# Two decode-state decays move from VectorE to GpSimd in a hybrid decoder step

## What is computed

```
# mixer A (HGRN2), one token per request
S_new = exp(b_last)[..., None] * S + einsum('bshk,bshv->bhkv', k * exp(b_last[:, None] - b), v)
# mixer B (mLSTM, the matrix memory)
a_c   = exp(F[:, -1] + m - m_new)
C_new = a_c[..., None, None] * C + einsum('bshk,bshv->bhkv', k * w[..., None], v)
n_new = a_c[..., None] * n + sum(k * w[..., None])
```

## Time and profile before

| | us |
|---|---|
| median of three runs | 1974.56 (1973.75 to 1975.65) |
| the profiled execution | 1974.06 |
| span of the profiled execution (first to last instruction) | 1972.0 |
| TensorE busy (89% of the span) | 1749.7 |
| VectorE busy (49%) | 960.1 |
| ScalarE busy (35%) | 693.6 |
| GpSimd busy (20%) | 386.5 |
| mean granted clock of TensorE | 0.903 of full |

### The profile page before, as it was taken

How to read it: one execution, slowest core, us unless ns; L and a number is a source line. 1 busy time by engine, 2 the same in 40 slices (tenths; PEclk the granted TensorE clock), 3 DMA queues, 4 the chain that set the end, 5 groups by cost and what they waited for, 6 DMA issues and landing times.

```text
span 1972.0 us, 33878 instructions
## 1 busy us (share of the span) xinstructions
PE 1749.7 (89%) x13564; PEld 1652.9 (84%) x13564; DVE 960.1 (49%) x1457; ACT 693.6 (35%) x1046; POOL 386.5 (20%) x234
## 2 busy tenths in 40 slices
PE   6999977579999999998999784776999999999994
PEld 6998945378999999998998562676999999999993
DVE  4676464542221122226764636335465465465484
ACT  4533353033221122235333431353344344344342
POOL 4302501033434343542015000203000000000031
PEclk8999975589999999999999755787999999999997
DMA  4212225022232222222123000237786786786782
GB/s 166 86 65 93 87 94 234 24 90 75 87 103 80 83 90 94 85 88 68 64 93 98 34 1 0 92 127 239 245 289 215 251 288 218 246 290 217 246 324 71
DMA packets 69274, 268.23 MB, mean 136 GB/s; under 512 B 11252, under 2 KB 11988, under 8 KB 68348
## 3 DMA queue, kind: packets, MB, share of 16 engines
q1 hardware_dynamic: 61152, 242.05, 35.8%
q10 hardware_dynamic: 4348, 15.89, 2.4%
q0 software_dynamic: 3648, 8.53, 1.2%
HBM read 250.09 MB, written 36.29 MB: 145 GB/s over the span
## 4 chain that ended last, share of the span: by engine, by line
PE 82%; DVE 10%; ACT 3%; issue 3%; DMA 1%; ACTq 1%; POOL 0%; DVEq 0%; POOLq 0%; SPq 0%
PE psum L1143 38%; PE psum L1190 11%; PE psum L1667 11%; PE psum L1677 10%; PE psum L1669 8%; PE psum L1195 1%; PE psum L1646 1%; DVE n L1738 1%; ACT a_pb L769 1%; PE psum L1635 1%; DVE r_ee L2132 0%; ACTq L959 0%; DVE r_bt L1934 0%; DVE acc L1725 0%; DVE a_lm L1804 0%
## 5 line engine op out<-in xcount | busy, mean ns | idle before, releaser
L1667 PE MATMUL psum<-xg,xhi 128*128 128x320 f32 x1408 | 376.7, 310 | 1.0 <-issue 0.5
L1669 PE MATMUL psum<-xg,xlo 128*128 128x256 f32 x1408 | 375.1, 281 | 0.0
L594 POOL TENSOR_TENSOR wlo<-wraw,whi 128x1024 fp32r<-128x1024 f32 (+1 forms) x90 | 230.5, 2563 | 349.6 <-ACT whi L730 349.6
L1667 PEld LDWEIGHTS psum<-xg,xhi 128*128 128x128 f32 x1408 | 265.4, 188 | 3.0 <-issue 2.8
L1669 PEld LDWEIGHTS psum<-xg,xlo 128*128 128x128 f32 x1408 | 264.6, 188 | 0.0
L1143 PE MATMUL psum<-xnh,whi 128*128 128x260 f32 x1120 | 234.8, 291 | 31.0 <-POOL xnl L647 13.4
L405 DVE TENSOR_TENSOR xlo<-xraw,xhi 128x1024 fp32r<-128x1024 f32 x176 | 215.1, 1223 | 58.5 <-ACT xhi L1091 58.4
L730 ACT CAST whi<-wraw 128x1024 fp32r<-128x1024 f32 (+1 forms) x130 | 140.7, 1085 | 290.4 <-DMA wraw<-in_w_in 166.4
L1091 ACT CAST xhi<-xraw 128x1024 fp32r<-128x1024 f32 x176 | 182.9, 1049 | 148.2 <-PE psum L1669 148.1
L1143 PE MATMUL psum<-xnh,wlo 128*128 128x260 f32 x1120 | 228.7, 286 | 0.0
L1143 PE MATMUL psum<-xnl,whi 128*128 128x260 f32 x1120 | 228.5, 286 | 0.0
(11 more groups left out here) (424 smaller groups left out, 2515.4 us busy)
## 6 DMA issues: line engine op xcount, KB each, us to landing
xraw<-in_moe_gu SPq DMA_DIRECT2D x176, 512.0 KB, 4.2
xraw<-in_moe_dn SPq DMA_DIRECT2D x64, 704.0 KB, 6.0
wraw<-in_w_in SPq DMA_DIRECT2D x54, 512.0 KB, 3.2
wraw<-in_ffn_gu SPq DMA_DIRECT2D x44, 512.0 KB, 3.3
wraw<-in_ffn_dn SPq DMA_DIRECT2D x16, 704.0 KB, 4.1
wraw<-in_w_out SPq DMA_DIRECT2D x16, 512.0 KB, 3.2
out_cache_s<-in_cache SPq DMA_DIRECT2D x4, 2040.0 KB
rows_in<-in_zero SPq DMA_DIRECT2D x8, 640.0 KB, 33.4
```

The source lines that it names most:

```text
L594: pool.tensor_tensor(wlo[u % RAW][:, 0:cols], wraw[u % RAW][:, 0:cols], whi[u % SPL][:, 0:cols].bitcast(F32), ALU.subtract).then_inc(lo_ma ...
L1667: pe.matmul(epart(n), xhi[n % HIX][:, k * P:(k + 1) * P], xg[:, k, :], start=(k == 0), stop=False, skip_group_check=True)
L1669: ins = pe.matmul(epart(n)[:, 0:256], xlo[n % RWX][:, k * P:(k + 1) * P], xg[:, k, 0:256], start=False, stop=(k == KD - 1), skip_group_che ...
```

## The change

Two products leave VectorE and go to GpSimd. The one on `S8` is put into GpSimd's stream between the clearing of `r_acb` and the low parts of the output weights, behind a wait for the loaded states and for the exponential of the decay. ScalarE takes that exponential in `mlstm` now, between `r_ec` and the cast of the output weights, where it was the first step of `sample`. The product on `C8` is put behind the low parts of the output weights and ahead of those of the mixed values, behind a wait for the PSUM bank of `aw` to be released. So that GpSimd has the decay in SBUF at that moment, VectorE copies `r_k` straight out of the PSUM bank, ahead of `diag(1)`; before it copied it from `r_aw` behind `diag(1)`. VectorE waits for `s8_decayed` ahead of the first outer product, and for `c8_decayed` ahead of the addition to column 64.

```
@@ GpSimd
                 step(pool.memset(R["rows"][:], 0.0))
                 bump(pool.memset(R["acb"][:], 0.0), S("rows_clear"), pool)
+                S8 = flat(TSK, 3 * NB * 64).rearrange("p (n d) -> p n d", d=64)
+                C8 = flat(TSV, 3 * NB * 65).rearrange("p (n d) -> p n d", d=65)
+                pool.wait_ge(state_in, 48 * (li + 1))
+                pool.wait_ge(S("f8_exp"), li + 1)
+                bump(pool.tensor_tensor(S8, S8, bc(R["ff"][:].rearrange("p f b -> p (f b)").unsqueeze(2), P, 3 * NB, 64),
+                                        ALU.mult), S("s8_decayed"), pool)
                 if li == 0:
                     for n in range(SPL):
                         lo(U_OUT[0] + n, KD * P)
                 else:
                     split_lo(pool, U_OUT[1], KD * P, lo_pool)
+                taken(pool, li, "aw")
+                bump(pool.tensor_tensor(C8, C8, bc(R["k8"][:].rearrange("p f b -> p (f b)").unsqueeze(2), P, 3 * NB, 65),
+                                        ALU.mult), S("c8_decayed"), pool)
@@ ScalarE, mlstm
                 free(act.copy(R["ec"][:, 3, :, :], ps[:, 3, :, 0:5]), li, "rt")
+                act.wait_ge(S("f8_copied"), li + 1)
+                sig(act.activation(R["ff"][:], R["ff"][:], ACT.Exp), "f8_exp")
                 for n in range(SPL):
                     hi(U_OUT[li] + n, KD * P)
@@ ScalarE, sample
-                act.wait_ge(S("f8_copied"), li + 1)
-                sig(act.activation(R["ff"][:], R["ff"][:], ACT.Exp), "f8_exp")
@@ VectorE, sample
                 v.wait_ge(state_in, 48 * (li + 1))
-                step(tt(S8, S8, bc(ff.unsqueeze(2), P, 3 * NB, 64), ALU.mult))
+                v.wait_ge(S("s8_decayed"), li + 1)
                 outer("vb", R["k8"][:].rearrange("p f b -> p (f b)"))
...
-                free(v.tensor_copy(R["aw"][:].rearrange("p f b -> p (f b)"), bank("aw")[:, 0:48]), li, "aw")
+                step(v.tensor_copy(R["aw"][:].rearrange("p f b -> p (f b)"), bank("aw")[:, 0:48]))
+                free(v.tensor_copy(R["k8"][:], bank("aw")[:, 0:48].rearrange("p (f b) -> p f b", f=3)[:, :, 0:NB]), li, "aw")
                 diag(1)
                 a8, w8 = R["aw"][:, :, 0:NB], R["aw"][:, :, NB:2 * NB]
                 step(tt(R["ff"][:], R["kh"][:, :, SEQ:T], w8, ALU.mult))
-                step(v.tensor_copy(R["k8"][:], a8))
-                step(tt(C8, C8, bc(R["k8"][:].rearrange("p f b -> p (f b)").unsqueeze(2), P, 3 * NB, 65), ALU.mult))
                 outer("vc", ff)
                 masked_query(R["bt"][:])
+                v.wait_ge(S("c8_decayed"), li + 1)
                 step(tt(C8[:, :, 64], C8[:, :, 64], ff, ALU.add))
```

## The result

| | before | after |
|---|---|---|
| median of 20 runs each, us | 1974.37 | 1979.40 |
| ratio to before, with its 95% interval | | 1.0025 (1.0018 to 1.0031) |
| the profiled execution, us | 1974.06 | 1976.98 |
| its span, us | 1972.0 | 1975.0 |
| mean granted clock of TensorE | 0.903 | 0.903 |

The change costs 0.25% of 1974.4 us, some 5.0 us (3.6 to 6.1). The forecast was 8.5 us. In the kernel after, VectorE's lines stand 9 further down, and TensorE's spread L1190 is L1199.

The account below looks back on a forecast made before the run. TensorE's wait for `diag(1)` was taken to bound the decode part, the decays being hidden by the spread. Copy 0.4, C8 7.1, S8 0.9 + 0.1 made 8.5 us more: 1983.1 us on the median, range 1975.8 to 1988.3.

Parts of the forecast that it names:

- What bounds: Decode part: TensorE waits for `diag(1)`; both decays on VectorE are hidden by TensorE's spread, so removing them gains 0.
- The copy of `r_k` ahead of `diag(1)`: VectorE, ahead of `diag(1)`: the moved copy adds 0.21 us to the chain, twice, 0.4 us.
- The decay of C8: GpSimd's 3.55 us product holds the second product of `diag(1)` on VectorE for its whole length, twice: 7.1 us.
- the lower end of 3.4 us: Shortest length allowed for GpSimd's C8 product, at 2.2 to 2.3 ns a column, "as in the 1024 row"; 3.55 us was taken.
- The decay of S8: GpSimd's product ahead of the low parts delays VectorE's chunk decays: 0.9 us in layer 0, 0.1 us in layer 1.
- the tie: Layer 1: S8's decay ends at 1144.55, the first chunk decay asks at 1144.52; 0.1 us or 2.35 us, 0.1 taken.
- The sum: Whole kernel: 0.4 + 7.1 + 0.9 + 0.1 = 8.5 us more, 1983.1 us on the median.
- the forecast's own: Range of the main forecast, 1981 to 1986 us: 3.4 to 3.8 us for a decay, either outcome in layer 1; chance 0.64.
- first rival: GpSimd's C8 decay runs only after `diag(1)`, holding none of its products: 1.4 us more, 1976.0 us; chance 0.17.
- GpSimd gets no turn during `diag(1)`: VectorE always goes first, or 8 partitions do not contend; 0.4 + 0.9 + 0.1 us are left, 1976.0 us; chance 0.17.
- The slower GpSimd: GpSimd needs 4.8 us for each decay with the repeated operand: 13.4 us more, 1988.0 us; chance 0.11.
- nothing collides: Neither decay on GpSimd holds VectorE up, only the copy of `r_k` is left: 1975.0 us; chance 0.04.

Follow-up runs that it names:

- e11: Kernel after, with GpSimd's two products taking a full-width second operand instead of the repeated decay; states come out wrong, another branch runs: 3880.86 us.
- e1: Only the S8 half of the change: the decay of C8 and its copy stay on VectorE as in the kernel before; 1.0004 of before.
- e2: Only the C8 half of the change: S8's product and its exponential stay as in the kernel before; 1.0027 of before.
- e3: Kernel after with one wait more: GpSimd's product on C8 also waits for the last product of `diag(1)`; 0.9996 of before.
- e9: Kernel before with `diag(1)` moved up and both query masks formed ahead of the outer products, decays on VectorE; 1959.28 us, 0.9919 of before.
- e7: Kernel before, decays on VectorE, with `diag(1)` moved up to where TensorE multiplies the query with S8; 1965.54 us, 0.9959 of before.
- e8: Kernel after, decays on GpSimd, with `diag(1)` moved up to where TensorE multiplies the query with S8; 1964.60 us, 0.9953 of before.

## Why the prediction was off by 3.5 us

**What bounds.** Right. `diag` was in nobody's shade and the decays were in the spread's. Taking them off gained nothing, seen in VectorE's idle times of 2.17 and 1.92 us and in the 5.78 us from the spread's start to the last outer product.

**The copy of `r_k` ahead of `diag(1)`, 0.4 us.** Right: 0.22 us in each layer.

**The decay of C8, 7.1 us.** Mechanism, place and turn-taking right, to the one product that is held; the size was not. The term measured 2 x 2.49 = 5.0 us. The step that failed is the length of GpSimd's product: 3.55 us was worked out for two full operands, and the repeated operand brought 2.80 us. That case had been put as a doubt upwards only (4.8 us); the lower end of 3.4 us was not low enough. Nor was that end the 1024 row's: its 2419 ns are 2.36 ns a column and would give 3.7 us. A further 0.3 us a piece went because the hold is shorter than the product: the trace shows GpSimd's end at 376.17 + 3.30 = 379.47, so at 2.80 us it began at 376.67, 0.17 us ahead of VectorE's issue at 376.84, and it let VectorE in at 376.84 + 3.17 - 0.68 = 379.33, 0.14 us ahead of its end. The rows of before had this: the chunk decay that ends at 307.44 takes 0.36 us by itself, so it began at 307.08, 0.14 us ahead of the low part's end at 307.22. The Trainium skill (GPSIMD Engine Reference, 3.1 Elementwise) has 4497 ns for an addition of two tensors with 2048 columns. Scaled to 1560 columns that is an estimate of 3.4 us, also 0.6 us more than the 2.80 measured; e11's product of C8 agrees with it, 3.97 us less the 0.50 us of waiting, but the repeated operand does not.

**The decay of S8, 0.9 + 0.1 us.** Wrong, for the most part by the same length. At 2.76 us it ends at 301.56, as the first chunk decay asks (301.42); at 3.50 us it would have ended at 302.30. So in layer 0 the change spares that chunk decay the 0.64 us for which a low part held it before, and the second is held no longer than before. From ScalarE's last copy into `r_ec` to VectorE's last chunk addition, layer 0 went from 14.72 us (298.74 to 313.46) to 14.34 us (298.20 to 312.54). In layer 1 the first chunk decay asked ahead of the end and lost 0.51 us, more than the 0.1 of the tie, which was drawn at the time at which it asked before; it asked sooner, 2.71 us behind ScalarE's last copy instead of 4.10. The same stretch shortened from 13.29 to 12.41 us all the same, with a granted clock of 0.63 instead of 0.55 between 1139 and 1155 us. e1 puts the whole half at 0.8 us (-1.2 to 2.8).

**The sum.** 0.44 + 4.98 + about 0 = 5.4 us, against 5.0 us measured (3.6 to 6.1). Of the 3.5 us too much, 2.1 are the C8 product and about 1 the S8 product; the rest is within the interval. The wide range (1975.8 to 1988.3) held the measured 1979.4 us, the forecast's own (1981 to 1986) did not. By the time alone the forecast could not have been told from its first rival: 1979.4 lies 3.7 us under 1983.1 and 3.4 us over 1976.0. The held product tells them apart.

**The rivals.** That GpSimd gets no turn during `diag(1)` fell with the held product, 3.17 us in both layers, and with e2. The slower GpSimd fell with the 2.80 us in e3. That nothing collides fell with e2 against e3: the same product costs 5 us in one place and nothing in another. That the decays were on the chain fell here, but it came true in e9, once `diag(1)` had gone and TensorE had its higher clock. That was the point from which this rival was said to decide.

## What to carry to other kernels

Before work goes to GpSimd, look at what VectorE runs in that moment: here an instruction with two SBUF operands on the chain paid for nearly all of a GpSimd product (2.49 of 2.80 us), and one with an operand in PSUM paid nothing. One wait can move the product from the one to the other, as in e3. And work that hides behind TensorE gives nothing when it leaves; move what TensorE waits for (`diag(1)`) into a time when VectorE waits for TensorE, which was worth 8 to 9 us in e7 and e8.

## What the runs showed of the hardware

- GpSimd's product of two tensors took 2762 ns for 1536 columns with an operand repeated 64 times along the last axis, 3446 ns with a full one.
- Separate partitions did not spare VectorE: a GpSimd product on partitions 64 to 127 held one of VectorE's on partitions 0 to 7 for 2.49 us, as long as one on all 128 did. No other split was run.
- TensorE ran the second spread at half clock in every trace in which it had stood idle for `diag(1)` ahead of it, 3.93 us in before, 4.26 us in e3, 6.65 us in after. Where `diag(1)` was early and the spread followed TensorE's work on S8 and the `aw` bank without a gap, it ran in some layers mostly at full clock (e7, layer 0) and in others at half (e7, layer 1). A window of e7 over the spread and the outer products of layer 0, then one over the first half's spread (columns as in the earlier trace rows):

```profile
377.30:381.50 4.20, 3.21 (x12) 0.81 (x11) 3.96 (x8) 0.00 (x0) 0.00 (x0) 0.83 0.00 0
362.20:368.00 5.80, 5.67 (x10) 1.24 (x10) 3.14 (x4) 0.00 (x0) 0.00 (x0) 0.50 0.00 1
```

The granted clock is 0.83 in the one, a mean over both of its levels (2.4 and 1.2 GHz), and 0.50, the lower one, in the other. The same matrix product took 0.59 us at the higher level and 1.06 us at the lower.
